# Prompt MLP by one level of Strassen's algorithm, and the second half's mixer output tiles in one run ahead of it

## The reference, cut to what matters

```
h   = rmsnorm(x, g_pre_mix);  p = h @ w_in          # 1024 -> 6 x 1024
A   = (B * causal_dwconv3(C * xv)) @ w_out_conv
Bp  = pool_scale * groupwise_linear(trailing_mean_w(u) - u)
mix = (sigmoid(gate_conv) * A + sigmoid(gate_pool) * Bp) @ w_o
x   = x + rmsnorm(mix, g_post_mix)
x   = x + rmsnorm(relu(rmsnorm(x, g_pre_mlp) @ w_up)**2 @ w_down, g_post_mlp)   # 1024 -> 4096 -> 1024
```

## Time and profile before

| | us |
|---|---|
| median of 3 runs | 1008.09 |
| lowest, highest | 999.15, 1008.79 |
| span of the profiled execution | 997.7 |
| spans of the 8 cores | 995.3 to 997.7 |

### The profile page before, as it was taken

How to read it: one execution, slowest core, us unless ns; L and a number is a source line. 1 busy time by engine, 2 the same in 40 slices (tenths; PEclk the granted TensorE clock), 3 DMA queues, 4 the chain that set the end, 5 groups by cost and what they waited for, 6 DMA issues and landing times.

```text
span 997.7 us, 15424 instructions; the slowest of 8 cores (995.3 to 997.7 us)
## 1 busy us (share of the span) xinstructions
PE 974.9 (98%) x5334; PEld 475.0 (48%) x5334; DVE 477.9 (48%) x804; ACT 308.9 (31%) x644; POOL 106.4 (11%) x121
## 2 busy tenths in 40 slices
PE   5899999999999999999999999999999999999997
PEld 3654444444554555454544444444445555544443
DVE  2567776764777666777365555101114344301012
ACT  2343432222444453333254444110113333201011
POOL 5520000000000000000000000002131000002021
PEclk7999999999999999999999999999999999999999
DMA  9599973263665761513857859973189954312132
GB/s 177 156 247 197 178 155 67 48 102 64 142 137 135 134 141 33 85 33 82 135 120 152 182 107 92 154 177 127 63 172 198 181 105 85 56 30 85 43 127 84
DMA packets 44956, 119.46 MB, mean 120 GB/s; under 512 B 21328, under 2 KB 21584, under 8 KB 40528
## 3 DMA queue, kind: packets, MB, share of 16 engines
q0 software_dynamic: 13104, 65.54, 41.1%
q1 hardware_dynamic: 31488, 52.64, 18.1%
q10 hardware_dynamic: 288, 0.30, 0.1%
HBM read 160.53 MB, written 19.01 MB: 180 GB/s over the span
## 4 chain that ended last, share of the span: by engine, by line
PE 89%; DMA 5%; DVE 3%; issue 1%; ACT 1%; POOL 1%; DVEq 0%; SPq 0%; ACTq 0%; POOLq 0%
PE PS L138 88%; DMA AR<-AR 3%; DVE AR L158 1%; ACT AR L155 1%; DMA AR<-w_down 1%; DMA AR<-x_p 1%; DVE AR L168 1%; PE PS L142 1%; POOL AR L163 1%; DVE AR L163 0%; DVE STAT L404 0%; POOL AR L129 0%; ACT STAT L155 0%; DVEq L223 0%; ACT ZO L155 0%
## 5 line engine op out<-in xcount | busy, mean ns | idle before, releaser
L138 PE MATMUL PS<-AR 128*128 128x512 bf16 (+1 forms) x5096 | 951.4, 348 | 1.8 <-DMA AR<-w_down 1.6
L138 PEld LDWEIGHTS PS<-AR 128*128 128x128 bf16 x5096 | 457.5, 98 | 484.7 <-issue 4.8
L155 ACT ACTIVATE AR<-PS 128x512 f32<-128x512 f32 (+3 forms) x222 | 130.2, 588 | 428.4 <-PE PS L138 396.9
L158 DVE TENSOR_TENSOR AR<-AR 128x512 bf16<-128x512 f32 (+7 forms) x264 | 171.5, 658 | 76.5 <-ACT AR L155 62.5
L404 DVE RECIPROCAL STAT<-STAT 128x1 f32<-128x1 f32 x67 | 10.7, 160 | 237.7 <-ACT STAT L155 237.2
L158 DVE TENSOR_TENSOR AR<-PS,AR 128x512 f32<-128x512 f32 (+1 forms) x122 | 73.6, 610 | 68.9 <-PE PS L138 52.9
L168 DVE SCALAR_TENSOR_TENSOR AR<-AR,CS 128x512 f32<-128x512 f32 (+1 forms) x80 | 53.7, 672 | 40.2 <-ACT AR L155 19.8
L155 ACT ACTIVATE AR<-PS,CS 128x512 f32<-128x512 f32 (+1 forms) x80 | 49.0, 621 | 76.6 <-PE PS L138 62.4
L155 ACT ACTIVATE AR<-AR,CS 128x512 f32<-128x512 f32 (+1 forms) x40 | 26.3, 658 | 105.5 <-DVE AR L158 105.5
L158 DVE TENSOR_TENSOR AR<-WPG 128x512 bf16<-128x512 f32 x53 | 36.6, 691 | 43.1 <-ACT WPG L155 43.1
L158 POOL TENSOR_TENSOR AR<-AR 128x1024 f32<-128x1024 f32 x16 | 37.4, 2348 | 163.4 <-DVE STAT L404 99.1
(11 more groups left out here) (40 smaller groups left out, 161.1 us busy)
## 6 DMA issues: line engine op xcount, KB each, us to landing
AR<-x_p SPq DMA_DIRECT2D x32, 512.0 KB, 8.2
AR<-w_up POOLq DMA_DIRECT2D x16, 1024.0 KB, 16.2
AR<-w_down POOLq DMA_DIRECT2D x16, 1024.0 KB, 12.8
AR<-w_m POOLq DMA_DIRECT2D x16, 768.0 KB, 8.7
x_d<-AR SPq DMA_DIRECT2D x17, 512.0 KB, 2.8
AR<-x_d SPq DMA_DIRECT2D x17, 512.0 KB, 5.3
y_p<-AR SPq DMA_DIRECT2D x16, 512.0 KB, 3.8
AR<-w_a POOLq DMA_DIRECT2D x24, 256.0 KB, 10.8
```

The costliest lines, as they stand in the source:

```text
L138: return self.add("pe", lambda e: e.matmul(out, lhsT, rhs, start=start, stop=stop), reads=[lhsT, rhs], writes=[out], signal=sig, name="mm")
L155: return self.add("act", lambda e: e.activation(out, in_, func, **kw), reads=rd, writes=wr, name=name)
L158: return self.add(eng, lambda e: e.tensor_tensor(out, in0, in1, op), reads=[in0, in1], writes=[out], name=name)
```

## The change

Each prompt half is now 1024 tokens by itself. h, w_up, the activations and w_down are cut into 2x2 blocks, and each block product of up and of down is done by 7 products in place of 8, in the Winograd form: sums of weight blocks (`up_sums`, `b_sum`) and of activation blocks (`h_sums`, `a_sum`) on VectorE in bf16; products that share a term are summed on in the same PSUM bank, which is read between them. `up_step` works on one weight block's new products between the previous one's old products. Down is `d_p1` and `d0` to `d6`, with four 128-token rows by 512 columns in banks at a time. The sample tile keeps all 8 products. Banks that live on are held (`grab`, `drop`). The output tiles 8 to 16 come in one run before the MLP, x1 is added on POOL for all tiles, and w_o has fixed chunks 8 to 15. The host cuts w_up and w_down anew. The MLP's loads are issued by hand (`load_up`, `load_dn`: 4 DMAs of 1 MB each). The diff, cut to its core:

```diff
-    def __init__(self, steps, loads, low_until):
+    def __init__(self, steps, loads):
...
-busy = [low_until] * LOW + [-1] * (NCH - LOW)
+busy = [len(steps)] * LOW + [-1] * (NCH - LOW)
...
-    for c in range(0, NCH - n + 1, 4 if n == 4 else 1):
+    at = loads[key].get("at")
+    for c in range(0, NCH - n + 1) if at is None else (at,):
         cand = (max(busy[c:c + n]), c)
         if best is None or cand < best:
             best = cand
...
 def bank():
-    b = min(range(8), key=lambda i: bank_used[i])
+    b = min((i for i in range(8) if i not in held), key=lambda i: bank_used[i])
     touch(b)
     return b
+held = set()
+def grab():
+    b = bank()
+    held.add(b)
+    return b
+def drop(b):
+    held.discard(b)
+    touch(b)
...
 for nh in range(2):
-    loads[("o", nh)] = dict(n=4)
+    loads[("o", nh)] = dict(n=4, at=LOW + 4 * nh)
...
     pm = pair(b2)
     ss = stat()
-    P.act(MTJ, pm, AF.Square, accum_out=ss, name="sq_mix")
+    xr, mt, mtj, hn = s_buf(i)
+    P.act(mtj, pm, AF.Square, accum_out=ss, name="sq_mix")
     rstd_from(ss)
-    P.stt("dve", MT, pm, ss, GPM, ALU.mult, ALU.mult, name="mixn")
+    P.stt("dve", mt, pm, ss, GPM, ALU.mult, ALU.mult, name="mixn")
     touch(b2)
     touch(b2 + 1)
-    P.tt("dve", XR[i % 3], MT, XR[i % 3], ALU.add, name="x1")
+    P.tt("pool", xr, mt, xr, ALU.add, name="x1")
 def s_b2(i):
-    x1 = XR[i % 3]
+    x1, mt, mtj, hn = s_buf(i)
     x1_store[i] = P.dma("sp", x1_d[i, :, :], x1, "x1s%d" % (i % 3), name="x1store")
     ss = stat()
-    P.act(HN[i % 6], x1, AF.Square, accum_out=ss, name="sq_x1")
+    P.act(hn, x1, AF.Square, accum_out=ss, name="sq_x1")
     rstd_from(ss)
-    hn = HN[i % 6]
     P.stt("dve", hn, x1, ss, GPL, ALU.mult, ALU.mult, name="hn")
-    if i + 3 < NT:
+    if i + 3 < NT and (i >= 8 or i + 3 < 8):
         load_xr(i + 3)
-    dst = h2T[:, :, i * 128:(i + 1) * 128]
+    dst = h_tile(i)
     key = "ts%d" % (i % 6)
     cnt = P.dma_cnt[key] = P.dma_cnt.get(key, 0) + 16
     P.add("sp", lambda e: e.dma_start_transpose(out=dst, in_=hn), reads=[hn], writes=[dst], name="xpose",
...
+def h_sums(half):
+    t1, t2, t3, t4 = (ts_at(half, i) for i in range(4))
+    P.tt("dve", t1, hq(half, 1), hq(half, 0), ALU.subtract, name="hs")
+    P.tt("dve", t2, hq(half, 3), t1, ALU.subtract, name="hs")
+    P.tt("dve", t3, hq(half, 3), hq(half, 1), ALU.subtract, name="hs")
+    P.tt("dve", t4, hq(half, 2), t2, ALU.subtract, name="hs")
...
+def load_up(half, b):
...
+    P.dma("pool", arv(L["raw"][b % 3], BF16, [3072]), w_up3[b], "ur%d" % (b % 3), name="wload")
+    P.dma("pool", arv(L["a22"][b % 4], BF16, [1024]), w_up1[b], "ua%d" % (b % 4), name="wload")
+def up_sums(half, b):
+    a11, a12, a21, a22 = (up_raw(half, b, i) for i in range(4))
+    s1, s2, s3, s4 = (up_s(half, b, i) for i in (1, 2, 3, 4))
+    P.tt("dve", s3, a11, a21, ALU.subtract, name="ws")
+    P.tt("dve", s1, a21, a22, ALU.add, name="ws")
+    P.tt("dve", s2, s1, a11, ALU.subtract, name="ws")
+    P.tt("dve", s4, a12, s2, ALU.subtract, name="ws")
+def up_mm(half, b, e, bk, wt, src, start):
+    for k in range(4):
+        P.mm(PS[:, bk, :], wt[:, 4 * e + k, :], src[:, k, :], start=(start and k == 0),
+             stop=(k == 3), chain=True)
...
+def relu_sq(eng, dst, x):
+    if eng == "act":
+        P.act(x, x, AF.Relu, name="relu")
+        P.act(dst, x, AF.Square, name="rsq")
+    else:
+        P.stt(eng, dst, x, 0.0, x, ALU.max, ALU.mult, name="rsq")
+def up_old(half, b, part):
+    for e in range(2):
+        u = 2 * b + e
+        bb = ub[(half, "b", u)]
+        if part == 6:
+            up_mm(half, b, e, bb, up_s(half, b, 2), ts_at(half, T_2), False)
+        elif part == 7:
+            up_mm(half, b, e, bb, up_s(half, b, 3), ts_at(half, T_3), False)
+        else:
+            up_mm(half, b, e, bb, up_raw(half, b, 3), ts_at(half, T_4), False)
+    for e in range(2):
+        u = 2 * b + e
+        bb = ub[(half, "b", u)]
+        if part == 6:
+            c = ubuf(half, "c", b, e)
+            P.tt("dve", c, PS[:, bb, :], c, ALU.add, name="C12")
+        elif part == 7:
+            q = ubuf(half, "q", b, e)
+            P.tt("dve", q, PS[:, bb, :], q, ALU.add, name="C22")
+        else:
+            P.act(ubuf(half, "t", b, e), PS[:, bb, :], AF.Relu, name="C21")
+            drop(bb)
+def up_fin(half, b, part):
+    for e in range(2):
+        u = 2 * b + e
+        if part == 6:
+            relu_sq("act", act_at(u, 2), ubuf(half, "c", b, e))
+        elif part == 7:
+            relu_sq("dve", act_at(u, 3), ubuf(half, "q", b, e))
+        elif part == 4:
+            t = ubuf(half, "t", b, e)
+            P.tt("pool", act_at(u, 1), t, t, ALU.mult, name="sq21")
+        else:
+            relu_sq("dve", act_at(u, 0), ubuf(half, "p", b, e))
+def up_new(half, b, part):
+    for e in range(2):
+        u = 2 * b + e
+        if part == 1:
+            bk = ub[(half, "b", u)] = grab()
+            up_mm(half, b, e, bk, up_raw(half, b, 0), hq(half, 0), True)
+        elif part == 5:
+            bk = ub[(half, "c", u)] = grab()
+            up_mm(half, b, e, bk, up_s(half, b, 1), ts_at(half, T_1), True)
+        elif part == 2:
+            bk = ub[(half, "a", u)] = grab()
+            up_mm(half, b, e, bk, up_raw(half, b, 1), hq(half, 2), True)
+        else:
+            up_mm(half, b, e, ub[(half, "c", u)], up_s(half, b, 4), hq(half, 3), False)
+    for e in range(2):
+        u = 2 * b + e
+        if part == 1:
+            P.copy("act", ubuf(half, "p", b, e), PS[:, ub[(half, "b", u)], :], name="p1")
+        elif part == 5:
+            P.copy("act", ubuf(half, "q", b, e), PS[:, ub[(half, "c", u)], :], name="p5")
+        elif part == 2:
+            p = ubuf(half, "p", b, e)
+            bk = ub[(half, "a", u)]
+            P.tt("dve", p, PS[:, bk, :], p, ALU.add, name="C11")
+            drop(bk)
+        else:
+            bk = ub[(half, "c", u)]
+            P.copy("act", ubuf(half, "c", b, e), PS[:, bk, :], name="p53")
+            drop(bk)
...
+    if o is not None:
+        up_old(half, o, 6)
+    if n is not None:
+        up_new(half, n, 1)
+    elif fill:
+        fill.pop(0)()
+    if o is not None:
+        up_fin(half, o, 6)
+        up_old(half, o, 7)
+        up_fin(half, o, 7)
+    if n is not None:
+        up_new(half, n, 5)
+    elif fill:
+        fill.pop(0)()
+    if o is not None:
+        up_old(half, o, 4)
+        up_fin(half, o, 4)
+    if n is not None:
+        if n + 1 < 8:
+            up_sums(half, n + 1)
+        up_new(half, n, 2)
+        up_fin(half, n, 2)
+        up_new(half, n, 3)
+        if half == 1:
+            up_sample(n)
+    for fn in fill:
+        fn()
+dn = {}
...
+def d_mm(bk, lhs, i, rhs, us, start, stop, sig):
+    for u in us:
+        P.mm(PS[:, bk, :], lhs(u)[:, i * 128:(i + 1) * 128], rhs(u), start=(start and u == us[0]),
+             stop=(stop and u == us[-1]), signal=(sig and u == us[-1]), chain=True)
+A_ = [lambda u, q=q: act_at(u, q) for q in range(4)]
...
+def d_p1(half, pc):
+    if pc == 0:
+        dn["b"] = [grab() for _ in range(4)]
+        if half == 1:
+            dn["sl"] = grab()
+    us = range(4 * pc, 4 * pc + 4)
+    for i in range(4):
+        d_mm(dn["b"][i], A_[0], i, lambda u: bq(half, 0, u), us, pc == 0, pc == 3, pc == 3 or i == 3)
+    if half == 1:
+        d_smp(half, dn["sl"], 0, 0, pc, pc == 0, False)
+    if pc == 3:
+        for i in range(4):
+            P.copy("act", t1v(half, i, 0), PS[:, dn["b"][i], :], name="p1")
...
+def a_sum(out_q, in0, in1, op):
+    for g in range(2):
+        P.tt("dve", out_q(8 * g, 8), in0(8 * g, 8), in1(8 * g, 8), op, name="as")
+def aq(q):
+    return lambda u, n: act_at(u, q, n)
+def b_sum(half, out, in0, in1, op, pieces=range(4)):
+    for pc in pieces:
+        P.tt("dve", bq(half, out, 4 * pc, 4), bq(half, in0, 4 * pc, 4), bq(half, in1, 4 * pc, 4), op, name="bs")
+def out_tile(half, i, x, xl, ydst_):
+    ss = stat()
...
+    rstd_from(ss)
+    P.stt("dve", x, x, ss, GPO, ALU.mult, ALU.mult, name="mlpn")
+    P.tt("pool", x, x, xl, ALU.add, name="y")
+    P.dma("sp", ydst_, x, "y%d" % (i % 4), name="ystore", is_output=True)
...
+def d0(half):
+    a_sum(lambda u, n: y_at(u, n), aq(2), aq(3), ALU.add)
+    a_sum(aq(2), aq(0), aq(2), ALU.subtract)
...
+def d1(half):
+    b_sum(half, 0, 1, 0, ALU.subtract)
+    a_sum(aq(0), lambda u, n: y_at(u, n), aq(0), ALU.subtract)
...
+        for i in range(n):
+            d_mm(dn["a"][i], A_[1], i, lambda u: bq(half, 2, u), us, pc == 0, pc == 3, pc == 3)
...
+        d_mm(dn["sl"], A_[1], 3, lambda u: bq(half, 2, u), range(16), True, True, True)
+    for i in range(4):
+        x = t1v(half, i, 0)
+        P.tt("dve", x, PS[:, dn["a"][i], :], x, ALU.add, name="C11")
+        drop(dn["a"][i])
...
+def d2(half):
+    a_sum(aq(1), aq(1), aq(0), ALU.subtract)
...
+        for i in range(n):
+            d_mm(dn["c"][i], y_at, i, lambda u: bq(half, 0, u), us, pc == 0, pc == 3, pc == 3)
...
+def d3(half):
```

(98 more changed lines are left out.)

309 lines of the change are left out of this document (184 added, 125 removed).

## The result

| | before | changed |
|---|---|---|
| median of 4 runs | 1006.89 us | 1022.19 us |
| lowest, highest | 999.15, 1008.79 | 1018.83, 1027.49 |
| span of the profiled execution | 997.7 | 1023.6 |

The ratio is 1.0188, 95% interval 1.0125 to 1.025: slower by 1.9%, and outside the range of 978 to 1020. The same kernel in two later comparisons on other chips gave 1016.51 (ratio 1.0148, 1.0084 to 1.0212) and 1016.47 us (1.0115, 1.0075 to 1.0154): inside the range, but slower than before both times.

The account below looks back on a forecast made before the run. The prediction took TensorE, busy for 98% of the span, to bound the kernel. Its terms summed to -5.3 us, giving 993.8 us like the profiled run or 1002.8 like the median; it forecast 998, range 978 to 1020.

Parts of the forecast that it names:

- Part 1: Prompt MLP, up and down: 256 fewer matmuls give -54.9 us, and the wait for w_down goes, -1.6.
- Rival E: Matmuls don't get fewer in time, for instance by waits in each chain of products: over 1029 us; chance 0.03.
- Part 2: Nine output tiles in one run: serial through ScalarE's queue, 7.4 us a tile against 3.4 of matmul, +43.2 us.
- Rival A: In the run, POOL and ScalarE overlap neighbouring tiles, PE stays at 3.4 a tile: -48.5, 951 us; chance 0.08.
- Part 3: Mixer with w_o pinned: its second half is issued later and lands late, +3.4 us (0 to +10).
- Part 4: Up loop: VectorE's bf16 weight sums are hidden by TensorE, cost 0, up to +6 us.
- Rival B: Weight sums run at the f32 price, in the down stage and the run: +35, 1029 us; chance 0.07.
- Rival C: Up loop and output tiles: VectorE falls behind as POOL's squares block it, +6 to +12 us; chance 0.17.
- Part 5: Down stage: waits of +1 and +1.8 us for VectorE's sums, slack over 3 us elsewhere, tail +0.5.
- Rival D: Down stage: weights land late, +5 to +25 us, 1000 to 1019; chance 0.13.
- The clock term: Behind the run: PE's pause leaves the granted clock lower for the next 4 us, +1.3 us (0 to 2).
- The number between: Whole kernel: 998 us, put between 993.8 (run like the profiled one) and 1002.8 (run like the median).

Follow-up runs that it names:

- e1: Changed kernel with ScalarE taking the Square of mix(i) before the Square of x1(i-1) in the run of tiles: 1008.43 us, ratio 1.0044.
- e2: Changed kernel with x1 of tiles 8 to 16 on VectorE in place of POOL: 1010.50 us, ratio 1.0044.
- a1: The changed kernel, unchanged, on a third chip: 1016.47 us, ratio 1.0115 against the kernel before.
- e7: e8's kernel but with x1 on POOL, and without the up loop's weight sums from block 2 on: 980.54 us, ratio 0.9771.
- e4: Changed kernel with four buffers in place of two for the x1 reloads of the down stage: ratio 1.0021.
- e10: Changed kernel with TensorE's pauses filled by identity matmuls, 14 ahead of each of tiles 9 to 16 and 108 ahead of the first products: 1017.54 us, ratio 1.012.
- b0: The kernel before, unchanged, profiled for its clock and spread of times: the profiled run took 1007.6 us.
- e3: The kernel before with only tiles 8 to 16 in one run ahead of its old MLP, their x1 on POOL: 1027.67 us, ratio 1.0235.
- a0: The changed kernel, unchanged, on a second chip: 1016.51 us, ratio 1.0148 against the kernel before.
- e9: e8 with the h sums moved out of the run, behind the first half's tiles: 972.80 us, ratio 0.9689.
- e8: Changed kernel with e1's order, e4's buffers, nine x and eight hn buffers, sums inside the run, later w_o, x1 of tiles 8-16 on VectorE: 977.31 us, ratio 0.9728.

## Why the prediction was wrong, step by step

The sum of -5.3 was made against the profiled execution. The spans differ by 1023.6 - 997.7 = +25.9, so 31.2 us are to be found. The first line of the table is the count of matmuls at the old pace, with the wait for w_down gone, and the last is what remains:

| term | forecast | measured | off |
|---|---|---|---|
| 256 matmuls, w_down wait | -56.5 | -56.5 | 0 |
| the run of nine | +43.2 | +44.1 | +0.9 |
| up to the run: w_o | +3.4 | +6.3 | +2.9 |
| waits in the MLP | +2.8 | +13.6 | +10.8 |
| tail | +0.5 | +4.2 | +3.7 |
| clock behind the run | +1.3 | +14.2 (rest) | +12.9 |

**Part 1** held: 256 matmuls less; at full clock 50 us hold 233 of them as before. Rival E is out.

**Part 2** held: a round of 7.4 us, P5 after 76.7 us where 75.8 were forecast, serial through ScalarE's queue. e1 and e2 cut a link each and shorten it; what stands behind it (x buffers, VectorE) came out only there. The prediction said that it would be wrong above all if the round weren't 7.4. The round was, and it was wrong elsewhere. Rival A is out by it. What the h sums cost in the run, +1.0 in the sum, was 2.3 (9.6 against 7.3).

**Part 3.** The pooling state's store is issued at 471.19 against 464.89, +6.3. Of it 2.2 are there already when w_o is issued, at 237.69 against 235.51 for the w_a that stood there: that comes from ahead of w_o's issue and not from the pinned chunks. 2.3 is the wait for w_o (a1: 4.1). The other 1.8 is what the half clock behind that wait costs: the granted clock is 0.96 from 244 to 248 us and 0.61 from 248 to 252, which is 1.7 us. The sum had the wait and not this. (The 9.9 us of landing in it stands in the earlier trace rows.)

**Part 4** held: the sums took 0.81, 1.27 and 2.43 us where 0.76, 1.36 and 2.57 were taken, and e7 shows them hidden. Rival B is out. Rival C's mechanism is there, as e1 showed, but cost the up loop nothing: from 574.74 to 780.6 TensorE has no wait. The Trainium skill, VectorE: DVE Perf Modes, section "The perf-mode tier table", has 1224 ns for 2048 elements; the trace's mean is 1266, so its rule holds. But the stalls that it was to take away were not those that came.

**Part 5 failed**, in the sentence "elsewhere slack is over 3 us". Neither of the two waits that it priced, +1 and +1.8, came. It counted VectorE's instructions and the banks, and not the DMA that one of VectorE's instructions waits for. `yl` frees no bank, so it was given no due time; but it stands ahead of the C sum that does. With two reload buffers its x1 is asked for one tile ahead, just when the next half's w_up is issued, and the reload takes 14.6 us in place of the median 5.3 of the earlier trace rows. 11.4 us of waits are there, 2.2 more in the second half's `d2` behind B sums that wait for their load, where the sum had 0; in the tail, which was given 0.5, the same buffers cost 4.2. e4 takes most of it back. Rival D was near: "weights late", +5 to +25. The weights were mostly on time; it was the x1 beside their loads that came late. That the loads are what slows a reload is read from the times: the six reloads issued within 7 us behind weight loads took 10.7 to 19.0 us, the other eleven 4.1 to 5.4.

**The clock term failed too**, not for what it named but for what it left out. Behind the run the granted clock was 0.50 until 575.4, which costs 1.6 us where 1.3 was forecast from the pause at the start of the kernel. Of the 14.2, 8.7 is 0.81, which no row of before showed and the sum had at nothing, and about 4.6 is half clock behind the two longer waits between the halves, so it comes with part 5's error. These estimates add up to 14.9. What brings 0.81 is open (on one chip the kernels with the products had more of it, e10's paragraph): a1, the same kernel on another chip, has none behind the run, and there the change costs 17.6 us of span, not 25.9.

**The number between.** The forecast added 4 us because before's median lay 9 over its profiled run. b0 shows such an execution, with w_down coming late on one core, in the MLP that the change replaces; the changed kernel's profiled run, 1024.65, is 1.0 us over its span. This step was unfounded, and moved the forecast toward the result by luck.

**What the change is worth.** Products and run are two changes. With the run's order, buffers and sums put right, and its pauses filled, the products give 0.965 of before's time (0.9612 to 0.9687, 970.20 us): -36 of the -54.9 that 256 matmuls are worth.

## What to carry to other kernels

Give every instruction of an in-order engine a due time, also one that frees nothing: what counts is what stands behind it, and when the DMA that it waits for is issued and beside what. Where work is packed into a run, write each engine's queue for one round and then ask for the second and third bound (buffers, then the engine without pauses), since removing the first gives only the distance to the next: 31 us were expected of e1, and about 10 came. And look at what the first matmul behind such a run needs from a full queue: P5's inputs lay ready before the run, but the sums of them were made in and behind it, while the same run ahead of the old MLP, which needs no sums, cost 22 us against 44 (e3; the link is argued).

## What the runs showed of the hardware

- The granted clock has a third level, 0.81, under full load: in stretches of 3.5 to 8 or of 15 us, on two or four neighbouring cores at about the same time (first profile, a0, b0, e9), in the kernel before as well (b0), and gone by itself with the load going on. In some executions it is absent (the profile of before, e10).
- An f32-input scalar_tensor_tensor on VectorE takes 3.4 us beside a POOL tensor_tensor of 2.34 (e1), and 1.28 alone; with that work on VectorE itself (1.23) hn is back at 1.28 (e8).
- A 512 KB reload issued half a microsecond behind 1 MB of weight loads took 14.6 us, against a median of 4.9 in the same run (first profile). Of its 17 reloads the six issued within 7 us behind weight loads took 10.7 to 19.0 us, the other eleven 4.1 to 5.4.
